# The sparse attention's projection of x: three split products against one whole float32 product, in a two-block transformer on one core

## What is computed

```python
h = x @ w_cols
h_gla, h_rwkv, h_nsa, h_vres = _split(
    h, (sum(GLA_COLS), sum(RWKV_COLS), sum(NSA_COLS), h.shape[-1] - IN_COLS))
...
q, kc, vc, ks, vs, kw, vw, gate = _split(h, NSA_COLS)
...
mix = jnp.concatenate([o_gla, o_rwkv, o_nsa], axis=-1) @ w_out[l]
x = _layer_norm(DEEPNORM_ALPHA * x + mix, ln1_w[l], ln1_b[l])
```

## Time and profile before

| what | value |
|---|---|
| median of three runs | 2303.24 us |
| the profiled execution | 2306.09 us |
| its span in the profile | 2304.3 us |
| mean granted clock of PE over the span | 0.981 |
| PE busy | 2211.7 us (96%) |
| DVE busy | 1529.1 us (66%) |
| ACT busy | 1108.2 us (48%) |
| b0 in the span | about 1246 to 1568 us |
| b1 in the span | about 1790 to 2090 us |

### The profile page before, as it was taken

How to read it: one execution, slowest core, us unless ns; L and a number is a source line. 1 busy time by engine, 2 the same in 40 slices (tenths; PEclk the granted TensorE clock), 3 DMA queues, 4 the chain that set the end, 5 groups by cost and what they waited for, 6 DMA issues and landing times.

```text
span 2304.3 us, 36385 instructions
## 1 busy us (share of the span) xinstructions
PE 2211.7 (96%) x14214; PEld 1948.8 (85%) x14214; DVE 1529.1 (66%) x2717; ACT 1108.2 (48%) x2003; POOL 422.3 (18%) x377
## 2 busy tenths in 40 slices
PE   6999999999999999999999998999998999999997
PEld 5888888988888888999888886888887987788886
DVE  5975765587678667766875685356766686456665
ACT  4654454365455443545554423246555533345554
POOL 2521001122122100012210140101213122001223
PEclk9999999999999999999999998899999999999999
DMA  6555432255555543134555411214554320203552
GB/s 239 194 176 163 150 125 76 81 192 180 188 190 188 178 150 118 45 103 152 192 168 184 135 49 40 83 37 147 190 186 142 134 84 20 103 28 119 187 179 93
DMA packets 88732, 310.31 MB, mean 135 GB/s; under 512 B 9840, under 2 KB 12144, under 8 KB 88048
## 3 DMA queue, kind: packets, MB, share of 16 engines
q1 hardware_dynamic: 88272, 305.29, 40.2%
q10 hardware_dynamic: 288, 2.69, 0.3%
HBM read 306.89 MB, written 1.05 MB: 134 GB/s over the span
## 4 chain that ended last, share of the span: by engine, by line
PE 91%; DVE 5%; ACT 2%; issue 1%; POOL 0%; DMA 0%; SPq 0%; DVEq 0%; ACTq 0%; POOLq 0%
PE ps L140 89%; DVE scratch L165 2%; PE ps L145 2%; ACT w_hi L154 1%; DVE w_lo L165 1%; DVE scratch L192 1%; ACT scratch L154 1%; DVE x L165 0%; POOL scratch L165 0%; DVE stats L182 0%; DMA ring<-in_w 0%; DVE scratch L177 0%; ACT scratch L191 0%; ACT h L154 0%; DVE scratch L204 0%
## 5 line engine op out<-in xcount | busy, mean ns | idle before, releaser
L165 DVE TENSOR_TENSOR w_lo<-ring,w_hi 128x1024 fp32r<-128x1024 f32 (+2 forms) x571 | 695.1, 1231 | 417.9 <-ACT w_hi L154 412.2
L140 PE MATMUL ps<-h,w_hi 128*128 128x512 f32 (+1 forms) x2784 | 871.5, 372 | 25.4 <-DVE h L177 18.6
L154 ACT ACTIVATE w_hi<-ring 128x1024 fp32r<-128x1024 f32 (+2 forms) x571 | 581.6, 1032 | 491.2 <-PE ps L140 484.1
L140 PE MATMUL ps<-h,w_lo 128*128 128x256 f32 x2448 | 686.8, 281 | 0.0
L140 PEld LDWEIGHTS ps<-h,w_hi 128*128 128x128 f32 x2784 | 505.0, 190 | 125.9 <-issue 22.7
L140 PEld LDWEIGHTS ps<-h,w_lo 128*128 128x128 f32 x2448 | 465.0, 190 | 0.0
L140 PE MATMUL ps<-f,w_hi 128*128 128x512 f32 (+1 forms) x1444 | 419.9, 357 | 3.1 <-DVE f L165 3.1
L140 PE MATMUL ps<-f,w_lo 128*128 128x256 f32 x1184 | 332.1, 280 | 0.0
L165 POOL TENSOR_TENSOR f<-f_work,f 128x256 fp32r<-128x256 f32 x132 | 187.6, 1422 | 591.5 <-ACT f L154 591.4
L140 PEld LDWEIGHTS ps<-f,w_hi 128*128 128x128 f32 x1444 | 255.6, 190 | 45.8 <-DVE w_lo L165 3.5
L140 PE MATMUL ps<-scratch 128*128 128x128 f32 (+9 forms) x1952 | 260.1, 303 | 8.3 <-DVE scratch L165 3.9
(11 more groups left out here) (136 smaller groups left out, 2210.6 us busy)
## 6 DMA issues: line engine op xcount, KB each, us to landing
ring<-in_w SPq DMA_DIRECT2D x520, 512.0 KB, 3.4
ring<-in_w SPq DMA_DIRECT2D x48, 384.0 KB, 3.5
ring<-in_w SPq DMA_DIRECT2D x16, 396.0 KB, 5.5
stage_consts<-in_ctwo ACTq DMA_DIRECT2D x1, 1344.0 KB, 5.8
stage_consts<-in_cthree ACTq DMA_DIRECT2D x1, 1281.0 KB, 5.4
ring<-in_w SPq DMA_DIRECT2D x9, 128.0 KB, 3.0
stage_consts<-in_cone SPq DMA_DIRECT2D x1, 1083.0 KB, 5.7
x<-in_x SPq DMA_DIRECT2D x4, 256.0 KB, 4.9
```

Source lines behind the costliest of these rows:

```text
L140: return self.e.matmul(out, lhsT, rhs, start=start, stop=stop, skip_group_check=free)
L154: return self.e.activation(out, x, func, **k)
L165: return self.e.tensor_tensor(out, a, b, op)
```

## The change

np calls a new function, pe_lin_whole, in place of pe_lin. It multiplies K.x itself (float32) with the raw unit (float32), one product where there were three: 16 in place of 48 per part. Its units are raw: no split on ACT or DVE, no pair of buffers, and their places in the ring are free when PE has used them. The waits on x are as before (the split of x is still made for the other projections). In the word of b1 one warm piece is taken from the start of the fourth line and one added further on in that line. The word of b0 stays.

```diff
 "b1":
-           "znnrzvrnrnrwuzrurwurvuwvumrvuvrvzwrzzzzzzzzvuwuuzvwvuwwvuuwvvzuwwvuuzwzvumwummzmzmzzmmmmmmzzzmmz"
+           "nnrzvrnrnrwuzrurwurvuwvumrvuvrvzwrzzzzzzzzzvuwuuzvwvuwwvuuwvvzuwwvuuzwzvumwummzmzmzzmmmmmmzzzmmz"
...
+def pe_lin_whole(e, K, ring, name, w, c0, m, need):
+
+    bk = [K.bank(e, ring, (name, tb)) for tb in range(2)]
+    per = UNIT // m
+    for k in range(8):
+        i = k % per
+        if i == 0:
+            u = K.unit(e, False, [(m, wtile(w, j, c0, m)) for j in range(k, min(k + per, 8))])
+            e.wait_ge(*K.loaded(u))
+        for n in need(k):
+            e.wait_ge(*n)
+        for tb in range(2):
+            ins = e.mm(bk[tb][:, 0:m], K.x[:, k, 128 * tb:128 * tb + 128], u.raw(i), k == 0, k == 7)
+            if k == 7:
+                ins.then_inc(*e.up("summed", (name, tb)))
+                K.released[u.n] = ("summed", (name, 1))
+            elif tb and (i == per - 1):
+                ins.then_inc(*e.up("unit_used", u.n))
...
     if what == "np":
         c, m = ((0, 512), (512, 396), (908, 396))[i]
-        pe_lin(e, K, GB, (s, "np", i), K.h, T.w, 0, 8, 8, NSA0 + c, m, xT)
+        pe_lin_whole(e, K, GB, (s, "np", i), T.w, NSA0 + c, m, xT)
```

## The result

The changed kernel takes 2320.73 us, the median of four runs (2319.0 to 2323.0), against 2304.35 (2302.55 to 2305.74) for the kernel before beside it: 16.4 us more, a ratio of 1.0071 with a 95% interval of 1.0059 to 1.0083. In a later session, beside other kernels, it took 2318.38 (2315.04 to 2321.22, five runs) against 2304.93, 1.0062 (1.0048 to 1.0077). The forecast was 2319.2.

What follows compares the result with a forecast made beforehand. PE, walking its list with few holes, was taken to bound the kernel. b0 +11.0 and b1 +5.0 gave +16.0 us on the profiled execution, 2319.2 us against the median; own range 2315 to 2323, 8 in 10 2310.5 to 2326.

Steps and rivals of the forecast that it cites:

- The np pieces on PE: np parts in both stages: float32 products priced by columns make PE's parts longer, 6.5 us per stage, 13.0 for both.
- What DVE and ACT lose: 24 splits leave each engine, 29 to 35 us of DVE and 23 of ACT, worth only the holes DVE ends.
- The holes: PE's waits for DVE that fewer splits close: 2.02 us before rkk and 0.1 before gl in b0, 1.45 before rbon in b1.
- the relief: Splits spared to DVE and ACT in both stages, counted hole by hole as 3.6 us gained, nothing after np 2.
- The new wait: b0 before rkk: DVE's early split of gl's second unit waits for a late load; +7.4 us, including np 0's 2.76.
- nothing is given back: b0 behind rkk: rbon and the warm pieces hang on rkk and do not shrink, so the +7.4 us stays.
- b1: Whole stage b1: no stall, longer np parts less 1.45 us gained before rbon, +5.0 us in sum.
- No stall: Rival, rkk of b0: load earlier or lists reach rg later; sum +9.3 us, 2312.6 us; chance 0.15.
- the stall: b0 before rkk: DVE stands at a blocked split, PE's hole grows from 2.0 to 6.7 us.
- The stall costs clock as well: Rival, around rkk of b0: the longer hole brings the half clock, +3.4 us, 2322.6 us; chance 0.15.
- DVE decides: Rival, behind np 2: DVE's backlog sets nq and nk, so 23 us would go, 2280 us; chance 0.05, including a part over 0.2%.
- It hides: Rival, b0 and b1: holes of 21 and 15 us take PE's 13, 2303 to 2306 us; chance 0.03.

Runs made afterwards that it cites:

- longer products alone: Kernel before with units split as before, but np makes one float32 product with the weights' rounded part; 9.3 us slower (6.5 to 14.1).
- b0 alone: Kernel before with whole float32 np products in stage b0 only, b1 keeping split products and its old word; 8.9 us slower (5.8 to 12.7).
- without the stall: Changed kernel with the split of gl's second unit in b0 put off to behind np 1; 2307.9 us, 3.5 us slower than the kernel before (1.6 to 6.2).
- np 1 alone: Kernel before with only np 1 made whole and raw in both stages, old word, gl's split in b0 put off; 4.3 us slower.
- b1 alone: Kernel before with whole float32 np products and the new word in stage b1 only; 2.4 us slower (0.9 to 6.0).
- rate probe: Kernel before with one or two short thrown-away products ahead of gate half (7,0) in f1, f3, f4 and f5; 4.2 us faster (2.8 to 8.1).
- relief alone: Kernel before with np units raw but 48 one-pass products per part kept, gl's split in b0 late; 10.5 us faster (6.7 to 13.6).
- wait alone: Kernel before, but ACT and DVE wait behind rg of b0 for the load of gl's second unit; time change between -4.1 and +1.4 us.

## Why the prediction was right

The total was 16.0 us by the forecast, 16.4 by the medians of the first session and 13.5 by the second. That the first came so near is in part luck: the 15.9 us of its profile hold 2.9 of f4's rate and 1.3 of clock in b1, which the forecast has not and the second profile has not either; that one is 13.3 us longer. By its steps:

- **The np pieces on PE.** Forecast 13.76 for np 0 and 10.64 for the others; measured 13.83 (13.74 in b1) and 10.72 to 10.74. Scaling one float32 product of 512 columns by columns is right to 1%. The rule of the Trainium skill (TensorE: Matmul & The Clock Gate, "Wait — 56ns, not 53.3ns?"), by which the removed products would have been shorter and the step dearer, was rightly not followed: the parts were 11.00 and 8.72 us.
- **What DVE and ACT lose.** DVE's 28.9 us were forecast as 29 to 35, ACT's 19.3 as 23, where all 24 splits had been priced at 1,024 columns. The holes: before rkk 2.02 forecast, 1.98 measured; before rbon of b1 1.45 forecast, 1.70 measured; before gl 0.1 forecast, 1.0 around gl measured (a longer np 1 closes that one by itself, as the longer products alone show). After np 2 nothing, as forecast. **This is the step that failed in size**, by what lies outside its holes: the relief by itself is worth 10.5 us (6.7 to 13.6) where 3.6 were counted, 4.7 of it in holes, 1.4 in clock that no longer falls before rbon, and for the rest no link to the relief was shown.
- **The new wait.** Place, cause and order of events are as forecast, +7.24 us at rkk against +7.4 and a hole of 6.4 against 6.7. That "nothing is given back" holds for the order of the pieces and left out the clock: 1.40 us more were lost up to rbon in both profiles of the changed kernel (none with b0 alone), 1.1 came back behind gO, and with the relief but without the wait 1.39 would have been won before rbon. The wait by itself is worth 9.3 us up to rbon in the profile, 8.0 with b0 alone, and 10 to 13 in the medians, against 6.7 forecast.
- **b1** has no stall, as forecast: +4.6 and +2.9 in the two profiles against +5.0. Its pieces and its hole are nearly as forecast (+2.7, -1.7, +2.1, +1.9). What the sum left out is clock: 1.9 us came back right behind np 2 in both, and 1.3 were lost before nc in the first alone.
- **The rivals.** *No stall* is refuted by the row, and its price was wrong too: without the stall the kernel takes 2307.9, not 2312.6. *The stall costs clock as well* came true in its mechanism. The clock was at half for 10.2 us from inside the wait on. The Trainium skill (TensorE: Matmul & The Clock Gate, "HAM oscillation — how this bites in real kernels") has the work behind a long wait start at the half clock, and the trace agrees: 0.50 when PE started rkk at 1319.85. Its price at this place was 1.4 us, not 3.4, as 3.85 of the 10.2 us lay inside the wait, and with b0 alone it was nothing. *DVE decides* is not so: the relief is worth 10.5 us, not 23, and less than the pieces grew, 13.5; with the stall taken out the change still costs 3.5 us (1.6 to 6.2). *It hides* is refuted by the products alone, +9.3 us.

So the sum held partly because two of its terms, of opposite sign, were both too small: the relief by some 7 us, the stall by 3 to 6. That they cancelled was luck.

No version here gets the relief for less than it is worth. Without its stall the change costs 3.5 us, with np 1 alone 4.3, in b1 alone 2.4. Of the kernels that compute all of np only the rate probe is clearly below the kernel before, and its gain has nothing to do with np. One was not run: np 1 alone with np 2's early splits in b1 put off as well.

## What to carry to other kernels

When a unit of work leaves a queue that others follow by a rule such as "four back" or "whoever held my place", look at what that rule now allows to be taken early, and at what is queued behind it: an early split that waits for a late load cost more here than any hole it had filled. And price a change on a cause by itself in both directions, as "longer products alone" and "relief alone" did; the total was right with two of its terms wrong.

## What the runs showed that was not expected

- PE's stream of fp32r products in the FFN stages runs at one of two rates, 2.773 or 2.827 us for 16 products, 2% apart, at full clock and without waits. One short product can switch it either way or not at all; one kernel showed either in f4 in two executions. A whole f4 or f5 in the slower one is 2.6 to 3.3 us longer. What decides the rate is open.
- The granted clock of stretches far from an edit changes from execution to execution and from kernel to kernel: from nc (1,0) of b0 to the start of f4 the shift is -3.8 us in three profiles, two of them with an unchanged b0, between -0.4 and 0.1 in eight, and +3.9 in one. It makes an edit of 2 us visible in the trace at its place and invisible in the time.
- Right behind rkk of b0 the half clock goes with the wait. The four kernels in which PE came to rkk without a wait have none there; the six with a wait of some 2 us have 3.4 us of it, the wait alone (4.3 us) 6.8, and the three profiles with 6.4 to 6.8 us have 6.8 or 10.2, part of it inside the wait.
